# Output projection of a hybrid encoder step: a tile's operands ahead of the next weight split, and a remainder ahead of the last stick

## The reference

```
xn = rms_norm(x, g_mix)
u, q, k, v, gate_a, gate_b = split(xn @ w_in)
a = multiscale_pool(u) -> per-group map -> * scale       # window means of 2, 4, 8, 16 minus the token
b = stick_breaking_attention(q, k, v)                     # 8 heads of 64, strictly causal
x = x + (sigmoid(gate_a) * (a @ w_pool_up) + sigmoid(gate_b) * (b @ w_sb_up)) @ w_out
x = x + square(relu(rms_norm(x, g_mlp) @ w_up)) @ w_down
x = x + sigmoid(rms_norm(x, g_ple) @ w_ple_gate) * (p @ w_ple_proj)
y = rms_norm(x, g_final)
```

## Time and profile before

| | us |
|---|---|
| median of 3 runs | 774.31 |
| lowest, highest run | 773.64, 775.06 |
| the profiled execution | 772.34 |
| its span | 770.6 |
| TensorE busy in the span | 754.8 |
| VectorE busy | 556.9 |
| ScalarE busy | 422.0 |
| GpSimd busy | 147.2 |

### The profile page before, as it was taken

One profiled execution on the slowest core, in us unless ns is written; L12 is line 12 of the kernel. 1 busy time (PEld: TensorE's weight loads), 2 busy tenths in 40 slices (PEclk: granted clock), 3 DMA queues, 4 the chain that ended last, 5 costly groups with the idle time before them and its releaser, 6 DMA issues.

```text
span 770.6 us, 14459 instructions
## 1 busy us (share of the span) xinstructions
PE 754.8 (98%) x5902; PEld 746.2 (97%) x5902; DVE 556.9 (72%) x705; ACT 422.0 (55%) x524; POOL 147.2 (19%) x259
## 2 busy tenths in 40 slices
PE   9999999999999999999999999999999999999994
PEld 9999999999999999999999999999999999999993
DVE  6776556566567527588998669965998667677986
ACT  7545535435485442477674347634763356556575
POOL 1051342453471332021110111111101000000001
PEclk9999999999999999999999999999999999999998
DMA  7254848769779899988797989789776957342503
GB/s 242 93 181 140 233 147 224 225 193 262 218 179 265 259 242 275 292 267 262 213 299 270 236 329 251 282 232 354 207 243 201 278 185 217 105 117 66 204 1 116
DMA packets 49516, 165.78 MB, mean 215 GB/s; under 512 B 6320, under 2 KB 8368, under 8 KB 49456
## 3 DMA queue, kind: packets, MB, share of 16 engines
q1 hardware_dynamic: 28512, 94.16, 35.6%
q0 software_dynamic: 18688, 67.18, 35.5%
q10 hardware_dynamic: 2256, 3.60, 1.4%
HBM read 160.39 MB, written 71.63 MB: 301 GB/s over the span
## 4 chain that ended last, share of the span: by engine, by line
PE 90%; DVE 5%; ACT 3%; issue 1%; DMA 1%; SPq 0%; POOL 0%; POOLq 0%; DVEq 0%
PE psum L1646 23%; PE psum L1697 16%; PE psum L1345 14%; PE psum L1351 14%; PE psum L1348 14%; PE psum L1394 1%; PE psum L1422 1%; DMA xt<-x_t 1%; PE psum L1420 1%; PE psum L1382 1%; PE psum L1381 1%; ACT xt L1265 1%; PE psum L1401 1%; PE psum L1406 1%; ACT L879 0%
## 5 line engine op out<-in xcount | busy, mean ns | idle before, releaser
L853 ACT ACTIVATE w_hi<-raw_more 128x1024 fp32r<-128x1024 f32 x83 | 87.7, 1056 | 72.3 <-PE psum L1697 43.3
L1345 PE MATMUL psum<-a_hi,w_hi 128*128 128x272 f32 x576 | 120.6, 291 | 0.6 <-DVE w_lo L1812 0.5
L1820 DVE TENSOR_TENSOR w_lo<-raw_more,w_hi 128x1024 fp32r<-128x1024 f32 x83 | 101.1, 1222 | 26.1 <-ACT w_hi L853 25.7
L1351 PE MATMUL psum<-a_hi,w_lo 128*128 128x272 f32 x576 | 119.3, 289 | 0.0
L1348 PE MATMUL psum<-a_lo,w_hi 128*128 128x272 f32 x576 | 118.9, 288 | 0.0
L1646 PE MATMUL psum<-u_hi,w_hi 128*128 128x272 f32 x560 | 116.4, 289 | 1.0 <-ACT h_of L1097 1.0
L1646 PE MATMUL psum<-u_hi,w_lo 128*128 128x272 f32 x560 | 115.8, 289 | 0.0
L1646 PE MATMUL psum<-u_lo,w_hi 128*128 128x272 f32 x560 | 115.7, 288 | 0.0
L1345 PEld LDWEIGHTS psum<-a_hi,w_hi 128*128 128x128 f32 x576 | 90.3, 189 | 1.1 <-DVE w_lo L1812 0.7
L1348 PEld LDWEIGHTS psum<-a_lo,w_hi 128*128 128x128 f32 x576 | 90.5, 189 | 0.0
L1351 PEld LDWEIGHTS psum<-a_hi,w_lo 128*128 128x128 f32 x576 | 90.0, 189 | 0.0
(11 more groups left out here) (287 smaller groups left out, 1553.0 us busy)
## 6 DMA issues: line engine op xcount, KB each, us to landing
sums_t<-w_tiles POOLq DMA_DIRECT2D x96, 512.0 KB, 8.2
raw<-w_tiles SPq DMA_DIRECT2D x63, 512.0 KB, 4.4
raw_more<-sums_t SPq DMA_DIRECT2D x42, 512.0 KB, 5.8
raw_more<-w_tiles SPq DMA_DIRECT2D x41, 512.0 KB, 4.5
sums_t<-sums_t POOLq DMA_DIRECT2D x32, 512.0 KB, 11.1
raw<-sums_t SPq DMA_DIRECT2D x22, 512.0 KB, 6.0
xt<-x_t SPq DMA_DIRECT2D x8, 272.0 KB, 5.7
y_t<-xt SPq DMA_DIRECT2D x16, 136.0 KB, 1.9
```

The costliest lines, as they stand in the source:

```text
L853: act.activation(w_hi[:, t % W_RING, :, :].rearrange("p k c -> p (k c)"), src, ACT.Copy)\
L1345: pe.matmul(base[:, h, :], w_hi[:, s, wk, :], at(hi, k, h * HALF, (h + 1) * HALF), start=(opens and q == 0), stop=False, skip_group_check= ...
L1351: mm = pe.matmul(base[:, h, :], w_lo[:, s, wk, :], at(hi, k, h * HALF, (h + 1) * HALF), start=False, stop=(closes and q == len(ks) - 1), s ...
L1820: dve.tensor_tensor(w_lo[:, t % W_RING, :, :].rearrange("p k c -> p (k c)"), src, w_hi[:, t % W_RING, :, :].rearrange("p k c -> p (k c)"), ...
```

## The change

In the output projection ScalarE now makes tile q's high operands first and splits the next weight tile behind them; VectorE likewise makes the low operands first and takes the weight remainder behind them (in the down projection, `nth` = 1, the order stays). In the last pair VectorE runs `group_lo(2)` ahead of `stick(1)`. No instruction is added or taken out.

```diff
@@ ScalarE, output projection @@
             ahead(T_OUT)
             for q in range(KT):
+                act.wait_ge(taken, N_OUT + q + 1)
+                operand_hi(0, q, g_mlp)
+
                 if q < KT - 1:
                     ahead(T_OUT + q + 1)
-                act.wait_ge(taken, N_OUT + q + 1)
-                operand_hi(0, q, g_mlp)
@@ VectorE, pair(i) @@
+                if last:
+
+                    group_lo(2)
                 stick(1, i)
                 if last:
-                    group_lo(2)
                     group_lo(3)
                     stick_later(1, i)
@@ VectorE, operand_lo(nth, q, t) @@
-                if q < KT - 1:
+                if nth and q < KT - 1:
                     ahead(t + 1)
                 dve.wait_ge(xg_done, KT * nth + q + 1)
@@ VectorE, output projection @@
             for q in range(KT):
                 add_residual(N_OUT + q, ORDER[q])
                 operand_lo(0, q, T_OUT + q)
+                if q < KT - 1:
+                    ahead(T_OUT + q + 1)
```

## The result

| | before | changed |
|---|---|---|
| median of 7 runs, us | 775.06 | 778.54 |
| lowest, highest | 773.64, 776.61 | 776.70, 779.32 |
| the profiled execution | 772.34 | 779.24 |

The ratio of the changed kernel to the one before is 1.0042, with a 95% interval from 1.0028 to 1.0055: 3.5 us slower.

The account below looks back on a forecast made before the run. TensorE, busy 98% of the span, was taken as the bound. Terms −0.25 (stick), +4.3 (chain lag) and +1.0 (clock) sum to +5.05 us on a 774.31 median, giving 779.4; range 776.8 to 781.4.

Parts of the forecast that it names:

- the clock's term: Third up product: TensorE's clock falls after about 3.7 us of idling, costing 1.0 us within bounds of 0 to 3.0.
- two load terms: Raw weight-tile loads in either kernel's output projection: the sum gave them no cost, taking loads not to bind.
- The chain: Output projection: residual add, operands, ScalarE's split, VectorE's split run serially; q = 7's add moves from 355.45 to 359.95.
- The steps: Output projection's serial steps: 5.35 us for an even q, 6.19 for an odd one, 11.54 a pair against TensorE's 12.08.
- the rule that ScalarE's copy starts 4.92 us: Up products: first product's copy starts 4.92 us after q = 7's residual add, lasts 0.60; third product starts after 0.1 handover.
- The chain's term: Third up product starts at 365.6, not 361.29, because the chain lags: 4.3 us, bounds 3.3 to 5.3.
- Where TensorE stands still: Up products: about 3.7 us idle ahead of the third, some 0.5 us stall in the first, within the 4.3 us.
- That margin of 0.32 us is all the slack there is: Up products: ScalarE's first copy ends at 360.97, third product starts at 361.29 in the same result slot.
- The loads don't bind: Output projection: raw tiles land before they are wanted, the next for 328.15 against 329.30.
- The load taken for the worst: SyncE's load behind q = 6's split: wanted at 371.50, 15.8 us left after moving; another load took 11.7 us.
- The assumption that the median lies 1.97 us above the execution: Whole kernel: 1.97 us added to the profiled execution's time to forecast the median, from 772.34 to 774.31.
- the 0.25 forecast: Last pair: `pool_part(0)` starts 0.52 us sooner, sums(1) gives back 0.2 to 0.3; net gain 0.25 us, bounds 0 and 0.52.

Follow-up runs that it names:

- e1: Kernel before with only `group_lo(2)` moved ahead of `stick(1)`, against the kernel before: 772.84 us, ratio 0.9966.
- e2: Kernel before with only the output projection's reordering, without the stick's edit, against the kernel before: 779.47 us, ratio 1.0046.
- e3: Changed kernel with ScalarE's loop in its old order (split first), VectorE's order as changed; against the kernel before: 782.45 us, ratio 1.0092.
- e5a: Changed kernel with GpSimd's weight-sum transfers left out from the sixth group on, against the kernel before: 776.46 us, ratio 1.0021.
- e6: Changed kernel with six unused constant matmuls on TensorE between projection and first up product, against the kernel before: 778.49 us, ratio 1.0040.
- e7: Kernel before, unchanged, profiled in another execution: 776.53 us; 41 runs in that job, 16 in 772.2 to 773.6 us, 24 in 774.7 to 776.6.
- e10: Kernel before with GpSimd's round of sums near 329 us held back until five projection tiles are done, against the kernel before: 772.85 us, ratio 0.9959.
- e8: Projection as changed but VectorE's weight remainder behind the next residual add, without the stick's edit; against the kernel before: 773.05 us, ratio 0.9985.
- e5b: Kernel before with GpSimd's weight-sum transfers left out from the sixth group on, against the unmodified kernel before: 772.63 us, ratio 0.9964.
- e4: Changed kernel with VectorE taking each weight remainder one step later, behind the next tile's residual add; against the kernel before: 772.15 us, ratio 0.9962.
- e9: Kernel before with only `group_lo(2)` moved ahead of `stick(1)`, run again, against the kernel before: 772.47 us, ratio 0.9979.

## Why the prediction was right, and where it was off

Direction, place and mechanism held: 778.54 lies in the range, forecast +5.05, measured +3.48. That the number came out so near owes something to luck: the clock's term cost nothing, and two load terms that the sum put at nothing nearly cancel.

The chain. The steps were right to 0.1 us, and so was the rule that ScalarE's copy starts 4.92 us and the third up product 5.6 us behind the q = 7 add: it held within 0.03 us in every run that lagged with VectorE's split in the place of either kernel (the change, e1, e2, e3, e5a, e6, e7, e10); in e8, with the split elsewhere, the third product comes 6.06 us behind that add. The chain's term, 4.3 us, measured 4.07 where no load disturbs. With loads, the third product of the changed kernel came 7.28 us later than before, and the chain's 4.07 with the 2.90 us of waits for raw tiles makes 6.97 of it; e2 and e6, with 3.38 and 2.26 us of such waits, came 7.71 and 6.57 us later, each again 0.2 to 0.3 us above that sum.

Where TensorE stands still. I put nearly all of it ahead of the third product; it came as 3.02, 0.58 and 1.53 us ahead of the first three. "That margin of 0.32 us is all the slack there is" overlooked the result slots: the first product needs the q = 6 add, the second the q = 7 add. That moved the waits and not the total, since the third product's start is set by the q = 7 add either way.

The clock. It fell, as forecast, and the 1.0 us for it was the term that failed: the first product ran 1.7 us longer for it, but the later waits hid that (e6), so it cost nothing. What a fall costs is decided by what TensorE waits for next. The rows, 0.50 from 358 and 1.00 from 362, agree with the rule of the Trainium skill (TensorE: Matmul & The Clock Gate, "What's actually happening"), fall and return.

The loads. "The loads don't bind" failed in both kernels. The load taken for the worst, issued at 353.25, was not the one: the last projection tile's was, issued at 332.85 in the changed kernel, wanted at 342.22 and there at 343.10. The changed kernel has 2.9 us of waits in its chain, and the kernel before loses 2.6 us in the median (e5b), which I missed because the profile I read was one of the executions in which the last raw tile landed early. The two nearly cancel. Split by the pair without transfers, 3.83 us is the chain less the stick's gain (776.46 − 772.63); the loads add 2.1 to the changed kernel (778.54 − 776.46) and 2.4 to the one before (775.06 − 772.63), which leaves the 3.5 measured. (The two pairs are of two jobs; the kernel before differs by 0.13 us between them.) The assumption that the median lies 1.97 us above the execution for reasons that both kernels share was wrong in the same way.

The stick. pool_part(0) gained 0.53 us, and the first two matmuls of sums(1) gave 0.18 back (the second comes 6.52 us behind pool_part(0), 250.70 − 244.18, and came 6.34 before, 251.43 − 245.09): 0.35 net against the 0.25 forecast. That the edit alone gains about 2 us was not forecast at all. That it moves SyncE's load closer to GpSimd's round is argued from single profiles and not shown: one of its two profiles has the late load.

## What to carry to other kernels

When two engines each do half of a split, moving both halves behind work in which the engines wait for each other makes one chain of everything; moving one of them a step on in the program keeps both covers (e4). Look for every slot that the following engine has to empty, not only for the last one. And one profile shows one order of landing: where an engine waits for a load in it at all, ask what another queue's transfer, issued a microsecond or two sooner or later, would do to the median.

## What the runs showed of the hardware

The load of the last projection tile (512 KB) kept ScalarE waiting in eight profiles (the change, e1 to e4, e6, e7, e8). There SyncE had issued it 1.9 to 5.7 us behind the start of GpSimd's round of sums, and ScalarE could begin on it 9.2 to 11.1 us after the issue (331.68 to 341.33 in e7, 330.93 to 340.18 in e1). Issued together with the round (330.50 in the first profile, in use at 336.85) or 0.7 us behind it (330.39 in e9, in use at 336.73), or with the round held back (e10, 332.36 to 338.71), it was there 6.4 us later at the latest. Between the first profile of the kernel before and e7, 2.2 us of difference in issue, the third up product moved by 3.05 us, counted from the projection's start. TensorE's granted clock was still 1.00 in the stretch in which work began again after 3.0 us of standing still, 0.50 in the two microseconds behind it, and 1.00 again from 362, with TensorE busy in between.
